# Squares of seven chunks added up on GpSimd, seven PSUM banks for the first feed-forward, wider mixer margins

## The chip, the cores and the metric

The kernel runs on the eight cores of one Trainium2 chip, each with four of the 32 sequences and without any exchange between cores. The time is that of the device, in microseconds (us), of the slowest core.

## What is computed

A macaron layer on x of shape (32, 2048, 1024): feed-forward, mixer of two attention groups, feed-forward, final norm. Weights are float32 in memory and bfloat16 in the matmuls.

```
h = x
h = h + 0.5 * swiglu(rmsnorm(h, g_ffn1), w_ffn1_gate, w_ffn1_up, w_ffn1_down)
u = rmsnorm(h, g_mix);  p = u @ w_in
o = concat(rmsnorm(mla(p), g_out_mla), rmsnorm(swa(p), g_out_swa))   # 8 heads each
h = h + o @ w_o
h = h + 0.5 * swiglu(rmsnorm(h, g_ffn2), w_ffn2_gate, w_ffn2_up, w_ffn2_down)
out = rmsnorm(h, g_final)
# rmsnorm(x, g) = x * rsqrt(mean(x*x) + 1e-6) * g;  swiglu = (silu(x@wg) * (x@wu)) @ wd, width 2816
```

## The kernel before

A core works on 16 tiles (NT) of 512 tokens, four per sequence. h lies transposed: 8 chunks of 128 features by 512 tokens in float32, with three buffers for h. For each tile there are FFN 1 (f = 0), the mixer, FFN 2 (f = 1) and the final norm. An FFN has 22 gate/up items (8 + 8 matmuls of 128x128 by 512 columns, L570 for the very first eight of a phase, L565 for the rest; tanh on ScalarE L580, two passes on VectorE L584 and L587) in two halves of 12 and 10, and after each half eight down items (L597; L604 adds the result to h). u, the normed input of an FFN, has one buffer, so it can be written only when the last gate/up item of the phase before has read it; eight down items of ten matmuls come behind that. The first two tiles go through FFN 1 together, with weights that are cast from float32 by GpSimd's DMAs on the way, in four quarters.

The norm of h (`pre_u` ahead of an FFN, in `mixer`, and in `final_out`) has this form: ScalarE squares a chunk into one of two buffers (sqF or sqM; L526, L711, L632), and `stat_mm` (L448) adds it up over the features on TensorE, with four matmuls that have the squares as weights and one column of 1/1024 as the moving operand. Eight chunks accumulate in one PSUM bank. VectorE then takes the reciprocal root with `newton` (L406 to L416, eleven operations on 128x4), and `bcast` (L425 to L435) writes it into diagonal matrices (dgF or dgM) that two matmuls (L435) spread over all partitions. VectorE scales h with it: L533 writes u, L719 the mixer's um, L640 the output.

PSUM has eight banks: FFNs turn over 0 to 2 (`fbank`), the mixer 3 to 6 (`mbank`), the norms use 7.

The order on each engine is made in advance. Every operation carries a planned duration (MM = 0.2185 per matmul, `d_act`, `d_dve`), a latency after it (LAT, 0.3 for GpSimd) and a due time vt; `Graph.schedule` is a list scheduler that takes on each engine, of the operations whose inputs are there in the plan, the one with the lowest vt. An FFN's operations have the running position fpos as vt, `pre_u` is due 20 ahead of it, and a mixer's operations are spread evenly over a window that ends 14 ahead of the tile's FFN 2. From then on each engine works through its list in that order, with semaphores for true dependences. The sequence of phases is FFN 1 of tile n, FFN 2 of tile n-1, and so on; the mixer of n fills in between.

```
            G.op("pe", [skey, ("onesc", oc)], [P(bank)], mm, 0.14)          # stat_mm
...
            pre_u(n, 16 * f, u1, ukey1, fpos[0] - 20)
...
                win[n] = (max(prev, phase_at[(0, n, "e")]), phase_at[(1, n, "s")] - 14.0)
```

GpSimd has only DMAs in its queue: the casting loads of the start, the outputs (outT) and the loads of x.

## Time and profile before

| | |
|---|---|
| median of 3 runs | 4984.26 us (4982.69 to 4986.34) |
| profiled execution, its time | 4978.47 us |
| its span, slowest core (core 2) | 4976.9 us |
| spans of the eight cores | 4958.9 to 4976.9 us |
| TensorE busy | 4827.9 us, 29209 matmuls recorded |
| VectorE busy | 2795.0 us |
| ScalarE busy | 1895.0 us |
| GpSimd busy | 91.2 us, 154 instructions |

The profile is of the slowest core of one execution. Engines are PE (TensorE matmul), PEld (its weight loads), DVE (VectorE), ACT (ScalarE), POOL (GpSimd) and SP (the queue of most DMAs). A share of busy time is a mean over the whole span, while the start, the long middle and the end have different limits, so it is read by stretches. Matmuls overlap, so their durations add up to more than the time between their starts. A few per cent of the matmul records are missing from this trace (29209 matmuls against 29784 weight loads). A wait is put down to the operation that came last.

### The profile page before, as it was taken

How to read it: one execution, taken by the hardware profiler on the slowest of the kernel's cores; microseconds unless marked ns; L12 is line 12 of the kernel's file. 1: busy time of each engine (PE TensorE's matmuls, PEld its weight loads, DVE VectorE, ACT ScalarE, POOL GpSimd, SP SyncE). 2: the span in 40 equal slices, each digit the busy share in tenths (PEclk: the TensorE clock that was granted, in tenths of full speed). 3: DMA queues.
4: the chain of work that ended last, by engine and by line, in shares of the span. 5: the costliest groups of instructions: out<-in, count | busy, mean ns of one | idle time of the engine just before them, and what ended most of it. 6: DMA issues, size and time to landing. Idle time of an engine off the chain costs nothing.

```text
span 4976.9 us, 93066 instructions; the slowest of 8 cores (4958.9 to 4976.9 us)
## 1 busy us (share of the span) xinstructions
PE 4827.9 (97%) x29209; PEld 2350.5 (47%) x29784; DVE 2795.0 (56%) x6313; ACT 1895.0 (38%) x3567; POOL 91.2 (2%) x154
## 2 busy tenths in 40 slices
PE   7899999999999999999999999999999999999998
PEld 3344444445444444544544444454544444445444
DVE  4366565555665565564557555555555655555654
ACT  1124425335233342534524243352642423336541
POOL 1100000000000000000000000000000000000000
PEclk9999999999999999999999999999999999999999
DMA  9985754544445454444445445444444545443434
GB/s 180 191 211 123 191 171 124 171 136 147 143 142 178 141 163 149 151 142 131 154 143 178 144 134 174 137 155 147 133 152 141 174 146 177 136 144 110 128 108 143
DMA packets 259288, 751.85 MB, mean 151 GB/s; under 512 B 28320, under 2 KB 36640, under 8 KB 258464
## 3 DMA queue, kind: packets, MB, share of 16 engines
q1 hardware_dynamic: 229664, 648.78, 41.9%
q0 software_dynamic: 28864, 97.07, 8.5%
q8 instruction: 258, 4.23, 0.4%
q14 instruction: 214, 1.75, 0.1%
q10 hardware_dynamic: 288, 0.03, 0.0%
HBM read 716.99 MB, written 73.92 MB: 159 GB/s over the span
## 4 chain that ended last, share of the span: by engine, by line
PE 92%; DMA 4%; DVE 2%; issue 2%; ACT 0%; SPq 0%; DVEq 0%; ACTq 0%; POOLq 0%; POOL 0%
PE ps L565 46%; PE ps L597 23%; PE ps L732 5%; PE ps L886 5%; PE ps L1039 4%; PE ps L906 3%; DMA sb_h<-xT 1%; PE ps L939 1%; PE ps L824 1%; DVE sb_u L533 1%; PE ps L435 1%; PE ps L448 1%; DMA sb_slotB<-wd 1%; PE ps L570 1%; PE ps L965 1%
## 5 line engine op out<-in xcount | busy, mean ns | idle before, releaser
L565 PE MATMUL ps<-sb_u,sb_slotA 128*128 128x512 bf16 x10390 | 2569.7, 380 | 33.4 <-DMA sb_slotA<-wgu 4.1
L565 PEld LDWEIGHTS ps<-sb_u,sb_slotA 128*128 128x128 bf16 x10688 | 999.1, 98 | 1077.2 <-issue 34.5
L597 PE MATMUL ps<-sb_act,sb_slotB 128*128 128x512 bf16 x5473 | 1311.0, 380 | 16.6 <-DMA sb_slotB<-wd 4.7
L584 DVE SCALAR_TENSOR_TENSOR sb_tb<-sb_tb,ps 128x512 f32<-128x512 f32 x704 | 483.0, 686 | 722.8 <-PE ps L565 322.6
L580 ACT ACTIVATE sb_tb<-ps 128x512 f32<-128x512 f32 x704 | 419.6, 596 | 1151.3 <-PE ps L565 927.5
L891 ACT ACTIVATE sb_PT<-ps 128x512 bf16<-128x512 f32 (+3 forms) x1280 | 653.4, 533 | 506.1 <-PE ps L886 364.0
L597 PEld LDWEIGHTS ps<-sb_act,sb_slotB 128*128 128x128 bf16 x5632 | 536.2, 98 | 608.4 <-issue 17.1
L587 DVE TENSOR_TENSOR sb_act<-sb_tb,ps 128x512 bf16<-128x512 f32 x704 | 482.7, 686 | 251.1 <-PE ps L565 212.5
L604 DVE SCALAR_TENSOR_TENSOR sb_h<-ps,sb_h 128x512 f32<-128x512 f32 x544 | 375.0, 690 | 409.2 <-PE ps L597 347.7
L886 PE MATMUL ps<-sb_QT,sb_KT 128*128 128x512 bf16 (+3 forms) x1225 | 407.1, 346 | 1.9 <-ACT sb_PT L891 0.7
L906 PEld LDWEIGHTS ps<-sb_VA,sb_PT 128*128 128x128 bf16 x4352 | 253.5, 98 | 193.4
L906 PE MATMUL ps<-sb_VA,sb_PT 128*128 128x65 bf16 x4352 | 294.5, 193 | 1.3
L732 PE MATMUL ps<-sb_um,sb_slotM 128*128 128x512 bf16 x1105 | 273.0, 380 | 7.3 <-DMA sb_slotM<-wms 6.4
L526 ACT ACTIVATE sb_sqF<-sb_h 128x512 bf16<-128x512 f32 x256 | 154.8, 626 | 246.9 <-PE ps L448 103.3
L1039 PE MATMUL ps<-sb_uo,sb_slotM 128*128 128x512 bf16 x962 | 229.8, 379 | 1.4 <-DVE sb_h L1043 0.4
L949 ACT ACTIVATE sb_PT<-ps 128x512 bf16<-128x512 f32 x248 | 146.0, 596 | 188.7 <-DVE ps L943 102.0
L943 DVE SCALAR_TENSOR_TENSOR ps<-ps,sb_Bb 128x512 f32<-128x512 f32 x248 | 169.3, 693 | 39.8 <-PE ps L939 38.1
L894 DVE TENSOR_TENSOR sb_PT<-sb_PT,sb_cmin 128x128 bf16<-128x128 bf16 x512 | 107.8, 221 | 138.4 <-ACT sb_PT L891 134.9
L533 DVE SCALAR_TENSOR_TENSOR sb_u<-sb_h,sb_gains,ps 128x512 bf16<-128x512 f32 x256 | 176.4, 740 | 10.2 <-PE ps L435 6.3
L732 PEld LDWEIGHTS ps<-sb_um,sb_slotM 128*128 128x128 bf16 x1112 | 108.8, 98 | 139.2 <-issue 9.5
L1043 DVE TENSOR_TENSOR sb_h<-ps,sb_h 128x512 f32<-128x512 f32 x128 | 88.4, 691 | 143.6 <-PE ps L1039 108.8
L886 PEld LDWEIGHTS ps<-sb_QT,sb_KT 128*128 128x128 bf16 x1280 | 124.4, 97 | 83.4 <-issue 1.8
(118 smaller groups left out, 2908.7 us busy)
## 6 DMA issues: line engine op xcount, KB each, us to landing
sb_slotA<-wgu2s SPq DMA_DIRECT2D x340, 512.0 KB, 3.5
sb_slotA<-wgu1s SPq DMA_DIRECT2D x308, 512.0 KB, 3.7
sb_slotM<-wms SPq DMA_DIRECT2D x318, 256.0 KB, 2.8
sb_slotB<-wd2s SPq DMA_DIRECT2D x120, 384.0 KB, 3.2
sb_slotB<-wd1s SPq DMA_DIRECT2D x112, 384.0 KB, 3.1
sb_slotB<-wd2s SPq DMA_DIRECT2D x124, 320.0 KB, 2.9
sb_slotB<-wd1s SPq DMA_DIRECT2D x112, 320.0 KB, 2.9
outT<-sb_h POOLq DMA_DIRECT2D x30, 1024.0 KB, 7.9
```

The source lines that it names most:

```text
L533: G.op("dve", [hk(n, kc), P(7), ("gains",)], ukey(kc), lambda kc=kc: nc.vector.scalar_tensor_tensor(out=ub[:, kc, :], in0=hc[:, kc, :], sc ...
L565: inst = nc.tensor.matmul(PS[bank][:], lhsT=w[:, a, kc, :], rhs=ub[:, kc, :], start=(kc == 0), stop=(kc == 7))
L580: G.op("act", [P(gb)], [("tb", t)], lambda: nc.scalar.activation(out=tb[:, t, :], in_=PS[gb][:], func=AF.Tanh, scale=0.5), d_act(512), vt=dv)
L584: G.op("dve", [("tb", t), P(gb)], [("tb", t)], lambda: nc.vector.scalar_tensor_tensor(out=tb[:, t, :], in0=tb[:, t, :], scalar=1.0, in1=PS ...
L587: G.op("dve", [("tb", t), P(ubk)], ak, lambda: nc.vector.tensor_tensor(out=act1[:, a0 + i, :], in0=tb[:, t, :], in1=PS[ubk][:], op=ALU.mul ...
L597: inst = nc.tensor.matmul(PS[bank][:], lhsT=w[:, c, :], rhs=act1[:, a0 + c, :], start=(c == 0), stop=(c == nch - 1))
L604: G.op("dve", [P(bank), hk(n, dc)], [hk(n, dc)], lambda: nc.vector.scalar_tensor_tensor(out=hc[:, dc, :], in0=PS[bank][:], scalar=0.25, in ...
L732: inst = nc.tensor.matmul(PS[b][:], lhsT=w[:, kc, :], rhs=um[:, kc, :], start=(kc == 0), stop=(kc == 7))
L886: G.op("pe", ktk(kti, hd) + [("Y", hd, 0), ("Y", hd, 1)], [P(b)], lambda: nc.tensor.matmul(PS[b][:, 0:N], lhsT=KT[:, kti, hd, kk * 128:(kk ...
L891: G.op("act", [P(b)], [("X", ps)], lambda: nc.scalar.activation(out=PT[:, ps, 0:N], in_=PS[b][:, 0:N], func=AF.Exp, scale=SC_MLA), d_act(N))
L906: inst = nc.tensor.matmul(PS[ob][:, j * 65:(j + 1) * 65], lhsT=PT[:, ps, (j - j0) * 128:(j - j0 + 1) * 128], rhs=VA[:, kb, hd, :], start=( ...
L1039: inst = nc.tensor.matmul(PS[b][:], lhsT=w[:, kc, :], rhs=uo[:, kc, :], start=(kc == 0), stop=(kc == 7))
```

## The change

A new function `h_stats` replaces the three places where squares went straight to TensorE. With `direct` nothing changes. Without it, the squares of chunks 0 and 1 are added on GpSimd into a float32 accumulator, those of chunks 2 to 5 are added to it one by one, and chunk 6 is added with the result in bfloat16 over the square itself; four matmuls take this sum of seven chunks and four more take chunk 7. The accumulator acF shares the place of dgF, and the mixer uses t2, the second half of wt. `direct` holds for tiles 0 and 1 ahead of FFN 1, for tiles 0, 1, 14 and 15 ahead of FFN 2 and in the mixer, and for the last output. While the first two tiles are in FFN 1, `fbank` turns over seven banks (0 to 6) in all quarters but the last. A mixer's window ends 45 ahead of FFN 2 for tile 0, 30 for tile 1 and 28 for the others, but for tiles 14 and 15, whose windows are set apart and stay; `pre_u` is due 24 ahead. GpSimd's addition is planned at D_POOL = 1.25. Behind the new function the lines of the changed kernel have higher numbers: stat_mm is L452, the additions are L468, L471 and L474, bcast's matmul is L439, L595 and L590 are gate/up and L622 is down.

```diff
--- before.py
+++ after.py
@@ -32,10 +32,12 @@
 NMP = 21
 NHS = 3
 FG = 2
+MARG = {0: 45.0, 1: 30.0}
 MAGIC = 1597463007.0
 
 
 MM = 0.2185
+D_POOL = 1.25
 LAT = {"pe": 0.33, "act": 0.22, "dve": 0.18, "pool": 0.3}
 SLACK_M = 0.6
 SLACK_E = 0.2
@@ -327,7 +329,9 @@
         Bb = sb("Bb", [128, 2, 8, 128], F32)
         sqF = sb("sqF", [128, 2, T], BF16)
         sqM = sb("sqM", [128, 2, T], BF16)
+        aF = here()
         dgF = sb("dgF", [128, 2, 4, 128], BF16)
+        acF = sb("acF", [128, T], F32, at=aF)
         dgM = sb("dgM", [128, 1, 4, 128], BF16)
         gains = sb("gains", [128, 43], F32)
         esink = sb("esink", [128, 8], F32)
@@ -451,6 +455,28 @@
                 return inst
             G.op("pe", [skey, ("onesc", oc)], [P(bank)], mm, 0.14)
 
+        def h_stats(n, sq, skey, acc, akey, bank, direct=False):
+
+            hc = h[n % NHS]
+            for c in range(8):
+                s = c % 2
+                G.op("act", [hk(n, c)], [(skey, s)], lambda c=c, s=s: nc.scalar.activation(
+                    out=sq[:, s, :], in_=hc[:, c, :], func=AF.Square), d_act(512))
+                if direct:
+                    stat_mm(sq, s, (skey, s), bank, 0, c == 0, c == 7)
+                elif c == 1:
+                    G.op("pool", [(skey, 0), (skey, 1)], akey, lambda: nc.gpsimd.tensor_tensor(
+                        out=acc, in0=sq[:, 0, :], in1=sq[:, 1, :], op=ALU.add), D_POOL)
+                elif 1 < c < 6:
+                    G.op("pool", [(skey, s)] + akey, akey, lambda s=s: nc.gpsimd.tensor_tensor(
+                        out=acc, in0=sq[:, s, :], in1=acc, op=ALU.add), D_POOL)
+                elif c == 6:
+                    G.op("pool", [(skey, 0)] + akey, [(skey, 0)], lambda: nc.gpsimd.tensor_tensor(
+                        out=sq[:, 0, :], in0=sq[:, 0, :], in1=acc, op=ALU.add), D_POOL)
+                    stat_mm(sq, 0, (skey, 0), bank, 0, True, False)
+                elif c == 7:
+                    stat_mm(sq, 1, (skey, 1), bank, 0, False, True)
+
 
         fpos = [0.0]
         phase_at = {}
@@ -458,8 +484,10 @@
         b_cnt = [0]
         f_bank = [0]
 
+        f_wide = [3]
+
         def fbank():
-            b = f_bank[0] % 3
+            b = f_bank[0] % f_wide[0]
             f_bank[0] += 1
             return b
 
@@ -517,15 +545,11 @@
             G.op("pe", reads, writes, fn, nmm * MM, vt=fpos[0] if vt is None else vt)
             fpos[0] += nmm * MM
 
-        def pre_u(n, gcol, ub, ukey, vt):
+        def pre_u(n, gcol, ub, ukey, vt, direct=False):
 
             G.vt = vt
             hc = h[n % NHS]
-            for c in range(8):
-                s = c % 2
-                G.op("act", [hk(n, c)], [("sqF", s)], lambda c=c, s=s: nc.scalar.activation(
-                    out=sqF[:, s, :], in_=hc[:, c, :], func=AF.Square), d_act(512))
-                stat_mm(sqF, s, ("sqF", s), 7, 0, c == 0, c == 7)
+            h_stats(n, sqF, "sqF", acF[:], [("dgF", 0), ("dgF", 1)], 7, direct)
             eps_in(PS[7][:, 0:4], [P(7)], nwF, 4, "nwF")
             newton(None, nwF, 4, "nwF")
             bcast(nwF, nwFb, "nwF", 0, 7, ("dgF",), dgF)
@@ -551,6 +575,7 @@
 
             def step(k, n, ub, uk, a0):
                 kind, grp, i = items[k]
+                f_wide[0] = 7 if len(tiles) > 1 and grp is not groups[-1] else 3
                 c_lo, nch = grp[0], grp[1]
                 view, keys = slots[k]
                 hc = h[n % NHS]
@@ -627,11 +652,7 @@
             si, ti = divmod(n, NTI)
             G.vt = vt
             hc = h[n % NHS]
-            for c in range(8):
-                s = c % 2
-                G.op("act", [hk(n, c)], [("sqF", s)], lambda c=c, s=s: nc.scalar.activation(
-                    out=sqF[:, s, :], in_=hc[:, c, :], func=AF.Square), d_act(512))
-                stat_mm(sqF, s, ("sqF", s), 7, 0, c == 0, c == 7)
+            h_stats(n, sqF, "sqF", acF[:], [("dgF", 0), ("dgF", 1)], 7, last)
             eps_in(PS[7][:, 0:4], [P(7)], nwF, 4, "nwF")
             newton(None, nwF, 4, "nwF")
             bcast(nwF, nwFb, "nwF", 0, 7, ("dgF",), dgF)
@@ -706,11 +727,7 @@
             R = [("R", j) for j in range(4)]
             G.dma("sp", "rope", [("pace", 0, 0, 16)] if n == 0 else [], [R[0], R[1]], rope[:].rearrange("p a t -> p (a t)"), rope_in[ti], 524288)
             bst = mbank()
-            for c in range(8):
-                s = c % 2
-                G.op("act", [hk(n, c)], [("sqM", s)], lambda c=c, s=s: nc.scalar.activation(
-                    out=sqM[:, s, :], in_=hc[:, c, :], func=AF.Square), d_act(512))
-                stat_mm(sqM, s, ("sqM", s), bst, 0, c == 0, c == 7)
+            h_stats(n, sqM, "sqM", t2, [W1], bst, n < 2 or n >= NT - 2)
             eps_in(PS[bst][:, 0:4], [P(bst)], nwM, 4, "nwM")
             newton(None, nwM, 4, "nwM")
             bcast(nwM, nwMb, "nwM", 0, bst, ("dgM",), dgM)
@@ -1069,13 +1086,13 @@
 
         late = [("A", i) for i in range(12, NFC)] + [("B", i) for i in range(8, 16)]
         PA, PB = late[:8], late[8:14]
-        pre_u(0, 0, u1, ukey1, -2000)
+        pre_u(0, 0, u1, ukey1, -2000, True)
         first_deps.update({0: [hk(0, 4)], 1: [hk(0, 5)], 2: [hk(0, 7)]})
         first_deps.update({i: [hk(1, min(7, 2 * i - 5))] for i in range(3, 8)})
 
         def second():
             load_x(1, 4, "sp", -4900, [hk(0, 7)])
-            pre_u(1, 0, u2, ukey2, -1500)
+            pre_u(1, 0, u2, ukey2, -1500, True)
         ffn(0, [one(0), two(1, 6)], QUARTERS, 3, {2: second})
         cast_first[0] = False
         a_ring[0] = ring_a
@@ -1103,7 +1120,7 @@
             if f == 1:
                 mixer(n)
                 m_cast[0] = False
-            pre_u(n, 16 * f, u1, ukey1, fpos[0] - 20)
+            pre_u(n, 16 * f, u1, ukey1, fpos[0] - 24, f == 1 and (n < 2 or n >= NT - 2))
             flush()
             b0 = fpos[0]
             lead[0] = LEAD_E if (f, n) in ((0, 2), (1, 0), (1, NT - 3), (1, NT - 2)) else 1000.0
@@ -1129,7 +1146,7 @@
         prev = 0.0
         for n in sorted(by_m):
             if n not in win:
-                win[n] = (max(prev, phase_at[(0, n, "e")]), phase_at[(1, n, "s")] - 14.0)
+                win[n] = (max(prev, phase_at[(0, n, "e")]), phase_at[(1, n, "s")] - MARG.get(n, 28.0))
             w0, w1 = win[n]
             prev = w1
             tot = 0.0
```

**What moves on TensorE at the start of FFN 2.** TensorE's rows at the end of an FFN 1 phase and the start of the FFN 2 phase behind it, in the middle of the program (a tile with the longest attention). sb_dgF is the diagonal matrix of the norm ahead of FFN 2, sb_sqM the squares of the next mixer's norm, sb_slotB_* down weights, sb_slotA_* gate/up weights. Before:

```order
L597 MATMUL ps<-sb_act,sb_slotB_72 128x512 x10
L435 MATMUL ps<-sb_dgF,sb_onesb 128x512
L597 MATMUL ps<-sb_act,sb_slotB_70 128x512 x5
L435 MATMUL ps<-sb_dgF,sb_onesb 128x512
L597 MATMUL ps<-sb_act,sb_slotB_70 128x512 x5
L448 MATMUL ps<-sb_onesc,sb_sqM 128x1 x4
L570 MATMUL ps<-sb_u,sb_slotA_68 128x512
L448 MATMUL ps<-sb_onesc,sb_sqM 128x1 x4
```

and with the change:

```order
L439 MATMUL ps<-sb_dgF,sb_onesb 128x512
L622 MATMUL ps<-sb_act,sb_slotB_72 128x512 x3
L439 MATMUL ps<-sb_dgF,sb_onesb 128x512
L622 MATMUL ps<-sb_act,sb_slotB_70 128x512 x10
L622 MATMUL ps<-sb_act,sb_slotB_71 128x512 x10
L622 MATMUL ps<-sb_act,sb_slotB_72 128x512 x10
L622 MATMUL ps<-sb_act,sb_slotB_70 128x512 x10
L622 MATMUL ps<-sb_act,sb_slotB_71 128x512 x10
L622 MATMUL ps<-sb_act,sb_slotB_72 128x512 x10
L622 MATMUL ps<-sb_act,sb_slotB_70 128x512 x10
L595 MATMUL ps<-sb_u,sb_slotA_68 128x512 x8
L590 MATMUL ps<-sb_u,sb_slotA_68 128x512 x8
```

The second dgF matmul has moved from five matmuls ahead of the first one that reads u to seventy ahead, and the groups of mixer squares that stood between the eight L570 have gone behind them.

**What moves on TensorE in the first feed-forward pair.** The squares of tile 2 (sb_sqF) and what stands around them; sb_slotK_* are four more gate/up buffers. Before, at the turn from the second to the third quarter:

```order
L597 MATMUL ps<-sb_act,sb_slotB_72 128x512 x12
L565 MATMUL ps<-sb_u,sb_slotK_95 128x512 x8
L448 MATMUL ps<-sb_onesc,sb_sqF 128x1 x12
L565 MATMUL ps<-sb_u,sb_slotK_96 128x512 x8
L448 MATMUL ps<-sb_onesc,sb_sqF 128x1 x8
L597 MATMUL ps<-sb_act,sb_slotB_71 128x512 x6
L448 MATMUL ps<-sb_onesc,sb_sqF 128x1 x4
```

and with the change, at the turn from the third to the fourth:

```order
L622 MATMUL ps<-sb_act,sb_slotB_72 128x512 x10
L622 MATMUL ps<-sb_act,sb_slotB_70 128x512 x10
L590 MATMUL ps<-sb_u_94,sb_slotA_67 128x512 x8
L452 MATMUL ps<-sb_onesc,sb_sqF 128x1 x8
L439 MATMUL ps<-sb_dgF,sb_onesb 128x512 x2
L622 MATMUL ps<-sb_act,sb_slotB_71 128x512 x17
```

They have moved back by some thirty rows, about a quarter of the pair, and the two dgF matmuls follow them at once.

**What GpSimd's queue holds in the middle of the program.** One output, the load of x behind it and the chain that comes next; sb_acF and sb_wt are the accumulators. Before, only the DMAs stood there. With the change:

```order
L474 TENSOR_TENSOR sb_sqF<-sb_sqF,sb_acF 128x512
L247 DMA outT<-sb_h_45 128x4x512 x2
L247 DMA sb_h_45<-xT 128x8x512
L468 TENSOR_TENSOR sb_acF<-sb_sqF 128x512
L471 TENSOR_TENSOR sb_acF<-sb_sqF,sb_acF 128x512 x4
L474 TENSOR_TENSOR sb_sqF<-sb_sqF,sb_acF 128x512
```

The six additions of a norm stand behind the load of x, which waits for the output ahead of it.

## Rows read from the trace of the kernel before

**Rows 1.** The page: busy time, and the chain that ended last, by engine.
```profile
PE 4827.9 (97%) x29209; PEld 2350.5 (47%) x29784; DVE 2795.0 (56%) x6313; ACT 1895.0 (38%) x3567; POOL 91.2 (2%) x154
...
PE 92%; DMA 4%; DVE 2%; issue 2%; ACT 0%; SPq 0%; DVEq 0%; ACTq 0%; POOLq 0%; POOL 0%
```

**Rows 2.** Stretches: length, busy us by engine, TensorE's clock, DMA share, GB/s.
```profile
150.00:250.00 100.00, 80.07 (x346) 34.04 (x352) 37.95 (x64) 11.42 (x20) 14.76 (x28) 0.88 0.92 196
...
600.00:700.00 100.00, 89.80 (x580) 43.10 (x591) 63.47 (x165) 42.63 (x82) 2.11 (x4) 0.93 0.45 127
...
800.00:4400.00 3600.00, 3566.34 (x21697) 1746.84 (x22124) 2042.21 (x4624) 1400.44 (x2620) 28.97 (x36) 1.00 0.48 150
...
1320.00:1325.00 5.00, 3.77 (x20) 1.91 (x22) 3.43 (x6) 2.85 (x5) 0.00 (x0) 0.67 0.17 66
```

**Rows 3.** TensorE's waits, 20 to 340 us: total us, times, longest.
```profile
PE ps L448 <- ACT sb_sqF L526: 10.0, 5, 5.4
PE ps L565 <- DVE sb_tb L584: 8.0, 5, 2.4
...
PE ps L597 <- DVE sb_h L604: 3.4, 3, 1.7
PE ps L597 <- DMA sb_slotB<-wd: 2.8, 2, 2.3
...
PE ps L565 <- DVE sb_h L604: 2.2, 2, 1.1
```

**Rows 4.** TensorE's waits, 340 to 800 us.
```profile
PE ps L732 <- DMA sb_slotM<-wms: 5.2, 2, 3.1
...
PE ps L570 <- DVE sb_u L533: 2.7, 7, 1.1
PE ps L448 <- ACT sb_sqM L711: 2.6, 6, 0.8
...
PE ps L435 <- DVE sb_dgF L432: 2.4, 1, 2.4
```

**Rows 5.** TensorE's waits, 800 to 4400 us.
```profile
PE ps L570 <- DVE sb_u L533: 7.7, 25, 0.7
PE ps L448 <- issue: 1.1, 3, 0.4
```

**Rows 6.** TensorE's waits, 4400 to 4977 us.
```profile
PE ps L435 <- DVE sb_dgF L432: 7.8, 3, 4.7
```

**Rows 7.** Groups of TensorE instructions by form: the stat matmuls.
```profile
L448 PE MATMUL ps<-sb_onesc,sb_sqF 128*128 128x1 bf16 x1536 | 83.3, 164 | 25.9 <-ACT sb_sqF L526 22.6 <-ACT sb_sqF L632 1.7 <-DVE sb_nwM L416 0.8
...
L448 PE MATMUL ps<-sb_onesc,sb_sqM 128*128 128x1 bf16 x704 | 41.1, 164 | 4.7 <-ACT sb_sqM L711 2.6 <-issue 1.1 <-ACT sb_sqM L755 0.9
```

**Rows 8.** TensorE's timeline, 1301 to 1324 us: start, length, operation, count.
```profile
1302.98 0.24 PE L448 MATMUL ps<-sb_onesc,sb_sqF 128*128 128x1 bf16 x4
1303.09 0.81 PE L1039 MATMUL ps<-sb_uo,sb_slotM 128*128 128x512 bf16 x3
1303.95 0.24 PE L448 MATMUL ps<-sb_onesc,sb_sqF 128*128 128x1 bf16 x4
1304.05 1.89 PE L1039 MATMUL ps<-sb_uo,sb_slotM 128*128 128x512 bf16 x8
1305.78 1.24 PE L597 MATMUL ps<-sb_act,sb_slotB 128*128 128x512 bf16 x5
```

**Rows 9.** Groups of VectorE and ScalarE instructions by form: busy us, mean ns.
```profile
L533 DVE SCALAR_TENSOR_TENSOR sb_u<-sb_h,sb_gains,ps 128x512 bf16<-128x512 f32 x256 | 176.4, 740 | 10.2 <-PE ps L435 6.3 <-PE ps L886 2.0 <-PE ps L906 1.7
...
L835 DVE TENSOR_TENSOR sb_qr<-sb_wt 128x512 bf16<-128x512 f32 x32 | 22.0, 687 | 1.8
...
L1092 DVE TENSOR_TENSOR sb_Bb<-sb_Bb,sb_mi 128x2048 f32<-128x2048 f32 x1 | 2.3, 2291 | 3.6 <-DMA sb_Bb<-bt 3.6
...
L526 ACT ACTIVATE sb_sqF<-sb_h 128x512 bf16<-128x512 f32 x256 | 154.8, 626 | 246.9 <-PE ps L448 103.3 <-DVE sb_h L1043 90.6 <-DMA sb_h<-xT 42.3
```

**Rows 10.** GpSimd's waits, the whole span.
```profile
POOL sb_h L245 <- DMA outT<-sb_h: 83.0, 10, 10.6
```

## The prediction

> **What bounds the kernel now.** First the page: TensorE is busy for 97% of the span and holds 92% of the chain that ended last [rows 1]. So a microsecond counts only if an instruction or a wait leaves TensorE's own queue. Second, the stretches [rows 2]: from 800 to 4400 us TensorE is busy for 3566 of 3600; time is lost ahead of 340 us, between 600 and 700, and behind 4400. The DMA engines are 92% busy between 150 and 250 us and 48% in the long middle. Third, TensorE's waits by stretch. In the first pair of feed-forwards it waits for squares, for PSUM banks that VectorE has not emptied (sb_tb, sb_h), but only 2.8 us for weights [rows 3]. From 340 to 800 it waits for the mixer's weights and for squares, dgF and u [rows 4]; in the middle almost only for u [rows 5]; at the end for dgF [rows 6].
>
> **Matmuls that go.** Before, 64 norms of h send eight squares each to TensorE, four 1-column matmuls per square (2048), and 16 mixers add 12 each for their latent norms: 2240, as the rows count them [rows 7]. Eleven of the 64 keep that form (two at the start, four before FFN 2, four in mixers, the last one). The other 53 (14 before FFN 1, 12 before FFN 2, 12 in mixers, 15 final) keep two groups of eight: 53 x 24 = 1272 matmuls less. Their price is not the 164 ns duration of the row, since matmuls overlap, but the time from the start of a group to the start of what follows: 1302.98 to 1303.09 and 1303.95 to 1304.05, so 0.10 to 0.11 us for four; I take 0.103 [rows 8]. (In the same rows eight 512-column matmuls go from 1304.05 to 1305.78, 0.216 each.) 318 groups x 0.103 = **33 us**, all of it on the bounding engine; no other cover exists. If groups also stop waiting for their squares it is more; that is in the next terms.
>
> The Trainium skill, page "TensorE: Matmul & The Clock Gate", section "LDWEIGHTS (loading the stationary operand)", gives a weight load of 128 columns about 107 ns; if these loads set the pace, 1272 of them would be worth an estimated 136 us. The trace disagrees: four loads and four matmuls pass in 0.11 us.
>
> **The middle: margins.** The mixer of a tile now ends 28 us ahead of its FFN 2 instead of 14 and the norm is asked for 24 us ahead instead of 20. The order shows what this does: before, the last dgF matmul stood one group ahead of the first matmul of FFN 2, with mixer squares between the eight that wait for u; now seven groups of ten (70 x 0.216 = 15 us) stand between, and the eight come in one row. The chain from dgF to a full u is eight L533 of 0.74 us with up to seven L604 passes of about 0.7 between, about 11 us [rows 9], so it fits in 15. That takes the waits on u (7.7) and the 1.1 of issue between them [rows 5], and most of the half clock behind the gap: 0.67 granted between 1320 and 1325, 3.3 us at 1.2 GHz [rows 2], costing half of itself, three times in the trace. I take **12 us** (8.8 of waits, the rest of clock). The same move for the early tiles (45 and 30 us) takes from 340 to 800 the waits on dgF (2.4), squares (2.6) and u (2.7) [rows 4]; the stretch 600 to 700 had a clock of 0.93, 14 us at the low level [rows 2], part of it behind this gap. I take **9 us**. The weight waits (5.2) stay. At the end the windows of the last two tiles keep their 14 us, and of the three waits on dgF, 7.8 us, the longest is 4.7, which I put down to the last output norm, where nothing changes [rows 6]: **2 us**.
>
> **The start: seven banks.** The waits on sb_tb and sb_h, 8.0 + 3.4 + 2.2, are three banks turning over when FFN 1 has only gate and up matmuls to issue; seven banks take them away. The squares' 10.0 us are tile 2's, whose x lands late; in the new order their matmuls stand in the last quarter of the pair, so this goes too [rows 3]. Ceiling 23.6 us, and some clock. But the weights come next: at 92% DMA share [rows 2] there is about 8% of the 240 us from 100 to 340 to catch up in, 19 us, and in the new order the two dgF matmuls stand right behind the two stat groups with nothing between, so a Newton chain of fourteen small VectorE operations plus dgF, some 6 us, can lie open there. I take **8 us** (ends: nothing, and 24).
>
> **GpSimd's additions: new.** 318 additions of 128x512, six in a chain per norm, each waiting for the one before. No row has one. Lower bound: VectorE's addition of two such operands from SBUF, 0.69 us; upper: its addition of four times the size, 2.29 us [rows 9]. I take the kernel's own table, D_POOL = 1.25, because its neighbours in that table match rows (the square is planned at 0.62 and takes 0.63, a VectorE pass 0.69 and 0.69) [rows 9]. Busy time costs nothing on an idle GpSimd; what counts is lateness, since TensorE's order is fixed and plans the stat group 1.55 us per addition (1.25 + 0.30) after the chain starts. If a step takes longer, TensorE stands. GpSimd's queue also holds the outputs and the loads of x; a load waits up to 10.6 us for the output ahead of it [rows 10], but in the order the next chain comes some 100 us of matmuls later. At the start, casting loads stand behind six additions on tile 2's squares, but later in the order than the place where TensorE waited for these squares before, so x should be there. Nothing for both. I put **8 us** for lateness, 53 chains x 0.15.
>
> Sum: -33 - 12 - 9 - 2 - 8 + 8 = **-56 us**. The profiled execution took 4978.5 (span 4976.9), so 4922; the median of the runs is 5.8 above it, so **4928 us**, 1.1% faster. (About 0.2%, 10 us, is what a measurement of this kernel can tell from no change.)
>
> **Rivals.**
> 1. *Only the matmuls go.* DMA takes back the start and new short waits the margins' gain: -33 to -38, so 4946 to 4951. For it: the DMA share of the start. Against it: the waits on u are VectorE's and the order puts 15 us before them. 20%.
> 2. *GpSimd is late; slower.* Place: the stat groups of the 53 norms. Where squares are all there (14 norms before FFN 1) six steps count; in the other 39 the chunks come 1.73 us apart or more (eight matmuls of 0.216) and only the last step counts, until a step is longer than 1.73; then all do. With a step of 1.55 + d the cost is (84 + 39) x d, plus 195 x (d - 0.18) beyond. Against a gain of 64 without lateness it decides from d = 0.31, a step of 1.86: with half of the table's 0.30 between two additions, an addition of about 1.7 us. At the upper bound, 2.29 + 0.15 per step, d = 0.89: 109 + 138 = 247, less 64, so 5167. At 1.8 us (d = 0.40): 49 + 43 - 64 = +28, 5012. For it: no row of the operation, and VectorE is 57% busy beside it (2042 of 3600 us) [rows 2]. Against: the table. 10%.
> 3. *Everything comes.* All 24 us of the start and some 5 of its half clock instead of 8, no lateness: -85, near 4900; half of both, 4912. For it: weights cost only 2.8 us of waits there. 12%.
> 4. *No effect:* the groups' cost is hidden otherwise. The row of 0.11 us speaks against it. 3%.
>
> The Trainium skill, page "GPSIMD Engine Reference", sections "Elementwise — side-by-side cycle accounting" and "Key points", gives a two-input GpSimd operation about 2.6 cycles per element, an estimated 1.11 us for 512 elements before overhead, sends elementwise work to VectorE instead, and says that GpSimd contends with VectorE operations that read two SBUF tensors. By the cycles alone the plan's step holds and rival 2 falls; by the contention it gains. No row here shows either.
>
> **Chances.** Forecast (4915 to 4942) 55%, rival 1 20%, rival 3 12%, rival 2 10%, rival 4 3%. Faster by over 0.2%: 0.87; within: 0.04; slower: 0.09. The range 4900 to 4962 takes in the forecast, rival 1 and most of rival 3, and leaves out rivals 2 and 4.
>
> **What would show it.** 968 stat matmuls on TensorE, and PE's waits from 800 to 4400 on u near nothing, with no half clock behind them. GpSimd with 318 TENSOR_TENSOR near 1.2 us each; waits of TensorE's stat line on GpSimd of under 10 us in all. No waits on sb_tb between 20 and 340, more on slotA or slotB. Wrong if the additions take over 1.7 us or stat matmuls wait on GpSimd by tens of microseconds, or if the first 340 us lose as much as before.

## The result, and the profile after

The change took **4912.7 us** (median of the first set of runs, 4895 to 4914; before 4985.1), 72 us less, where 56 were forecast; the ratio over these executions is **0.9844 [0.9818, 0.9871]**. A second set, the same kernel at another time (first experiment below), gave 4897 us and 0.9815 [0.9797, 0.9832], about 90 us less than before. Medians and ratios here and below leave out executions in which a die had a lower clock throughout. Part of the difference between the two sets is one stretch of 160 us in the profiled execution of the first, in which cores 0, 1, 6 and 7 had a clock of 0.81: they ended at 4907 to 4911 us, the other four at 4881 to 4885.

The page of the change, its slowest core: busy time, and the chain that ended last, by engine (before: [rows 1]).

```profile
PE 4832.4 (98%) x28512; PEld 2318.2 (47%) x28512; DVE 2803.2 (57%) x6313; ACT 1904.4 (39%) x3567; POOL 457.3 (9%) x472
...
PE 95%; DMA 3%; DVE 1%; issue 1%; POOL 0%; SPq 0%; ACT 0%; DVEq 0%; POOLq 0%; ACTq 0%
```

TensorE's part of the last chain went from 92% to 95%. The stretches of the change, core 1 (length; busy us of PE, PEld, DVE, ACT, POOL; granted clock; DMA share; GB/s). The same stretches of before are in [rows 2].

```profile
150.00:250.00 100.00, 87.22 (x365) 37.28 (x364) 40.95 (x69) 13.55 (x23) 21.71 (x34) 0.87 1.03 213
600.00:700.00 100.00, 99.58 (x595) 47.66 (x594) 75.42 (x202) 41.89 (x77) 16.06 (x16) 1.00 0.58 162
800.00:4400.00 3600.00, 3599.40 (x21208) 1735.24 (x21206) 2085.61 (x4711) 1411.82 (x2624) 353.30 (x318) 1.00 0.49 152
1320.00:1325.00 5.00, 5.00 (x25) 2.27 (x24) 3.26 (x5) 0.02 (x1) 0.00 (x0) 1.00 0.35 105
224.00:384.00 160.00, 158.64 (x709) 68.66 (x708) 92.79 (x178) 40.64 (x76) 8.37 (x16) 0.81 0.72 185
```

And the last of them on core 2 of the same execution:

```profile
224.00:384.00 160.00, 157.03 (x888) 74.33 (x887) 111.32 (x232) 56.54 (x114) 8.89 (x17) 1.00 0.78 205
```

In the long middle TensorE now stands still for 0.6 us of 3600, and the stretch 600 to 700 has its full clock. For before, [rows 2] is not the right row to compare with: it is of core 2, whose trace lacks 2% of the matmul records there (21697 matmuls beside 22124 weight loads). Core 1 of the same execution is complete, and idle for 10.6:

```profile
800.00:4400.00 3600.00, 3589.41 (x22114) 1745.39 (x22112) 2042.57 (x4623) 1399.99 (x2618) 28.98 (x36) 1.00 0.48 150
```

From 224 to 384 us, core 1 of the change got 709 matmuls through and core 2 888; it ended 28 us later.

TensorE's waits after, four stretches (20 to 340, 340 to 800, 800 to 4400, 4400 to 4977 us), total, times, longest. Before: [rows 3 to 6].

```profile
PE ps L590 <- DVE sb_tb L609: 8.3, 2, 8.0
PE ps L439 <- DVE sb_dgF L436: 4.8, 1, 4.8
PE ps L595 <- DVE sb_u L557: 1.6, 3, 1.2
...
PE ps L749 <- DMA sb_slotM<-wms: 11.8, 2, 6.1
...
PE ps L595 <- DVE sb_u L557: 1.3, 3, 0.6
...
PE ps L1056 <- DMA sb_slotM<-wms: 0.3, 1, 0.3
...
PE ps L439 <- DVE sb_dgF L436: 8.7, 2, 4.7
PE ps L885 <- DVE sb_KT L880: 2.2, 3, 0.9
```

GpSimd's additions, groups by form (busy us, mean ns | idle before):

```profile
L471 POOL TENSOR_TENSOR sb_acF<-sb_sqF,sb_acF 128x512 f32<-128x512 bf16 x164 | 190.7, 1163 | 190.2 <-ACT sb_sqF L463 186.3
L471 POOL TENSOR_TENSOR sb_wt<-sb_sqM,sb_wt 128x512 f32<-128x512 bf16 x48 | 55.9, 1165 | 3.6 <-ACT sb_sqM L463 1.9
L474 POOL TENSOR_TENSOR sb_sqF<-sb_sqF,sb_acF 128x512 bf16<-128x512 bf16 x41 | 47.7, 1163 | 58.8 <-ACT sb_sqF L463 58.2
...
L468 POOL TENSOR_TENSOR sb_acF<-sb_sqF 128x512 f32<-128x512 bf16 x41 | 47.3, 1155 | 3072.1 <-ACT sb_sqF L463 982.3 <-PE ps L1056 763.9 <-PE ps L439 560.3
```

An addition takes 1.16 us; the plan had counted 1.25 and 0.30 of latency, a step of 1.55. From start to start, an addition that reads the result of the one just before it comes 1.30 us behind it at the earliest, so this is the real step of a chain; where additions of two chains alternate, starts are 1.12 us apart. No wait of TensorE on GpSimd is in the lists, on any core. The estimate of 1.11 us worked out in the prediction from the Trainium skill, page "GPSIMD Engine Reference", section "Elementwise — side-by-side cycle accounting", stands 5% under the 1.16 of the rows: it agrees.

**Where the time went, by stretch.** The floor is the sum over TensorE's matmuls of the usual spacing of their starts where nothing waits: columns at 2.4 GHz plus 2.8 ns (0.216 us for 512), and 25 ns for one column. Lost time is what the spacing of their starts has beyond it, waits and low clock together, taken as the mean over the cores whose records are complete (us).

| Run | Floor | 0 to 340 | 340 to 800 | 800 to 4350 | 4350 to end |
|---|---|---|---|---|---|
| before | 4808.8 | 58.5 | 38.8 | 17.9 | 27.5 |
| the change, first set | 4777.0 | 46.9 | 29.0 | -1.8 | 25.6 |
| the change, second set | 4777.0 | 42.6 | 25.5 | -1.8 | 26.2 |

(-1.8 of 3550 is how exact the floor is.) From before to the second set: 32 matmuls, 16 the start, 13 the stretch to 800, 20 the middle, 1 the end, together 82; the spans of the slowest cores (4976.9 and 4895.4) differ by the same 82. (The second set's own comparison gives 93, 4990 less 4897: the profiled execution of before is from the first set, and with 4978 it was faster than the other four there.)

### The profile page after: what moved, and what is told of

Read it like the earlier page. It is cut to its first block, busy times and chain, and to the rows that moved or that the text cites. A ratio compares the mean times of both kernels' runs of the same rounds, so it can differ in the third digit from the quotient of the medians.

```text
span 4911.1 us, 91964 instructions; the slowest of 8 cores (4880.6 to 4911.1 us)
## 1 busy us (share of the span) xinstructions
PE 4832.4 (98%) x28512; PEld 2318.2 (47%) x28512; DVE 2803.2 (57%) x6313; ACT 1904.4 (39%) x3567; POOL 457.3 (9%) x472
## 3 DMA queue, kind: packets, MB, share of 16 engines
q1 hardware_dynamic: 229664, 648.78, 42.6%
## 4 chain that ended last, share of the span: by engine, by line
PE 95%; DMA 3%; DVE 1%; issue 1%; POOL 0%; SPq 0%; ACT 0%; DVEq 0%; POOLq 0%; ACTq 0%
PE ps L590 47%; PE ps L622 24%; PE ps L749 5%; PE ps L903 5%; PE ps L1056 4%; PE ps L923 3%; PE ps L841 1%; PE ps L956 1%; PE ps L595 1%; PE ps L439 1%; DMA wd1s<-sb_slotB 1%; PE ps L982 1%; PE ps L813 1%; PE ps L1030 1%; DMA sb_slotM<-wms 0%
## 5 line engine op out<-in xcount | busy, mean ns | idle before, releaser
L590 PE MATMUL ps<-sb_u,sb_slotA 128*128 128x512 bf16 x10688 | 2605.6, 381 | 1.0 <-DVE sb_PT L911 0.3
L590 PEld LDWEIGHTS ps<-sb_u,sb_slotA 128*128 128x128 bf16 x10688 | 1007.9, 98 | 1090.1 <-issue 48.4
L622 PE MATMUL ps<-sb_act,sb_slotB 128*128 128x512 bf16 x5632 | 1324.3, 381 | 2.6 <-DMA sb_slotB<-wd 1.4
L609 DVE SCALAR_TENSOR_TENSOR sb_tb<-sb_tb,ps 128x512 f32<-128x512 f32 x704 | 483.4, 687 | 634.7 <-PE ps L590 324.9
L622 PEld LDWEIGHTS ps<-sb_act,sb_slotB 128*128 128x128 bf16 x5632 | 539.3, 98 | 615.9 <-issue 26.3
L903 PE MATMUL ps<-sb_QT,sb_KT 128*128 128x512 bf16 (+3 forms) x1280 | 426.5, 348 | 0.2
L463 ACT ACTIVATE sb_sqF<-sb_h 128x512 bf16<-128x512 f32 x384 | 236.3, 626 | 364.1 <-DVE sb_h L1060 168.0
L468 POOL TENSOR_TENSOR sb_acF<-sb_sqF 128x512 f32<-128x512 bf16 x41 | 47.3, 1155 | 3072.1 <-ACT sb_sqF L463 982.3
L749 PE MATMUL ps<-sb_um,sb_slotM 128*128 128x512 bf16 x1112 | 276.6, 384 | 13.1 <-DMA sb_slotM<-wms 11.8
L471 POOL TENSOR_TENSOR sb_acF<-sb_sqF,sb_acF 128x512 f32<-128x512 bf16 x164 | 190.7, 1163 | 190.2 <-ACT sb_sqF L463 186.3
L911 DVE TENSOR_TENSOR sb_PT<-sb_PT,sb_cmin 128x128 bf16<-128x128 bf16 x512 | 119.1, 244 | 140.8 <-ACT sb_PT L908 136.9
```

Of the source, the lines that this page charges most:

```text
L463: G.op("act", [hk(n, c)], [(skey, s)], lambda c=c, s=s: nc.scalar.activation(out=sq[:, s, :], in_=hc[:, c, :], func=AF.Square), d_act(512))
L590: inst = nc.tensor.matmul(PS[bank][:], lhsT=w[:, a, kc, :], rhs=ub[:, kc, :], start=(kc == 0), stop=(kc == 7))
L609: G.op("dve", [("tb", t), P(gb)], [("tb", t)], lambda: nc.vector.scalar_tensor_tensor(out=tb[:, t, :], in0=tb[:, t, :], scalar=1.0, in1=PS ...
L622: inst = nc.tensor.matmul(PS[bank][:], lhsT=w[:, c, :], rhs=act1[:, a0 + c, :], start=(c == 0), stop=(c == nch - 1))
L749: inst = nc.tensor.matmul(PS[b][:], lhsT=w[:, kc, :], rhs=um[:, kc, :], start=(kc == 0), stop=(kc == 7))
L903: G.op("pe", ktk(kti, hd) + [("Y", hd, 0), ("Y", hd, 1)], [P(b)], lambda: nc.tensor.matmul(PS[b][:, 0:N], lhsT=KT[:, kti, hd, kk * 128:(kk ...
```

## Experiments

All edits are made to the changed kernel, unless a sentence says otherwise. Each set of runs had the kernel before beside it on the same chip. Times over the change are against the second set.

### The change again

The changed kernel without an edit, the reference for the next three.

> The changed kernel again, unaltered, beside the kernel before on the same chip. In its profile cores 0, 1, 6 and 7 had a stretch of 160 us from 223 us on with a granted clock of 0.81 and ended 25 us behind the other four (4881 to 4885). If that stretch belongs to the kernel's order, some cores show it in nearly every execution and the slowest core is near 4911; if it is chance of the execution, executions without it end near 4890. Ratio to before 0.982 to 0.986 either way.

Measured: 4897 us (4892 to 4900) against 4990 for before on that chip, ratio 0.9815 [0.9797, 0.9832]. The change is worth some 90 us where no stretch at 0.81 falls into it; the profiled execution has none on any core, so the kernel's order does not bring it by itself.

### All squares back on TensorE

```
 def h_stats(...):
-                if direct:
+                if True:
```

> The change with every norm's squares straight to TensorE (no addition on GpSimd); seven banks and margins stay. Theory: the 1272 matmuls come back at 0.103 us per four, +33 us, less the 8 us stall of 164 us, in which ScalarE's tanh stands behind squares that wait for GpSimd: undisturbed cores near 4884 + 25 = 4909, 2240 stat matmuls. Rival: GpSimd's additions cost nothing at the start and save waits of the stat groups too, then +33 to +45 (4917 to 4929).

Measured: 4941 us, 0.9904 [0.9889, 0.992]: 44 us over the change. The floor is 31.8 us higher, and lost time is 43.1, 34.3, 0.0 and 31.5 by stretch. So the margins alone clear the middle: TensorE is busy 3597.95 of 3600 us there. The rest is in the stretch to 800 (9 more than in the second set) and the end (5); since two profiles of one kernel differ by 3.5 and 0.6 there, how much of these is the edit's stays open. The GpSimd part carries about half of the change's 90 us, once margins and banks are there.

### Old margins

```
-MARG = {0: 45.0, 1: 30.0}
+MARG = {}
...
-            pre_u(n, 16 * f, u1, ukey1, fpos[0] - 24, ...)
+            pre_u(n, 16 * f, u1, ukey1, fpos[0] - 20, ...)
...
-                win[n] = (..., phase_at[(1, n, "s")] - MARG.get(n, 28.0))
+                win[n] = (..., phase_at[(1, n, "s")] - MARG.get(n, 14.0))
```

> The change with the margins of before (14 for all tiles, norm due 20 ahead). Theory: the margins are worth 19 us from 800 to 4400 (waits on u and half clock behind them) and up to 19 between 340 and 800: undisturbed cores near 4884 + 30 = 4914, waits on u from 800 to 4400 back to 8 us or more. Rival: the fewer stat groups between the matmuls that read u did it, and the margins alone are worth under 10 us: 4884 to 4894. Second rival: with the old margins the longer GpSimd chain is late and it costs more than before, over 40 us.

Measured: 4952 us, 0.9927 [0.9911, 0.9943]: 55 us over the change. Lost time by stretch: 46.2, 34.7, 35.8, 33.6. TensorE's waits in it, 800 to 4400 us:

```profile
PE ps L595 <- DVE sb_u L557: 11.0, 32, 0.9
PE ps L439 <- DVE sb_dgF L436: 8.9, 12, 1.2
PE ps L452 <- DVE sb_u L557: 2.4, 6, 0.4
```

That is more than before had in the same stretch [rows 5], and there is a wait on dgF that before had none of. With the old margins the longer chain through GpSimd ends too late, and TensorE waits for what comes behind it (the Newton steps, dgF, u), not for the sum itself. The margins are worth 38 us in the middle with the GpSimd sums, and 18 without (before 17.9, all on TensorE with the new margins 0.0). They are two things at once: a gain of their own and the price of the GpSimd chain.

### Three banks for the first FFN

```
-                f_wide[0] = 7 if len(tiles) > 1 and grp is not groups[-1] else 3
+                f_wide[0] = 3
```

> The change with three banks for the first pair. Theory: the waits on sb_tb and sb_h of 13.6 us come back and part of the half clock, +10 to +20 on undisturbed cores (4894 to 4904). If the stretch of clock 0.81 comes from the denser start, it is absent here and the slowest core is no slower than 4904, so the kernel as a whole gains; rival: the stretch is as frequent here, slowest core 4920 to 4930.

Measured: 4911 us in two executions, 14 over the change; no interval. Lost time ahead of 340 us is 59.4 against 42.6, everything behind it as in the change. Its waits, 20 to 340 us:

```profile
PE ps L590 <- DVE sb_tb L609: 25.3, 6, 9.3
PE ps L590 <- DVE sb_h L629: 3.0, 3, 1.1
```

Three banks with the GpSimd sums lose as much at the start as before did (58.5), so the start's whole gain is the banks'.

### Tile 2's first norm without GpSimd

With seven banks a wait of 8 us on sb_tb was still there. The rows of the change around it, core 1: GpSimd, then ScalarE, then VectorE, then TensorE (start, length, operation, idle before and what ended it).

```profile
160.22 0.53 POOL L247 DMA_DIRECT2D sb_slotB<-wd  x1 [14.02 <-PE ps L622]
...
161.86 1.06 POOL L247 DMA_DIRECT2D sb_slotM<-wm  x2
162.92 1.18 POOL L468 TENSOR_TENSOR sb_acF<-sb_sqF 128x512 f32<-128x512 bf16 x1
...
164.20 1.15 ACT L463 ACTIVATE sb_sqF<-sb_h 128x512 bf16<-128x512 f32 x2 [12.78 <-POOL sb_acF L468]
...
169.83 0.58 ACT L605 ACTIVATE sb_tb<-ps 128x512 f32<-128x512 f32 x1
...
170.51 0.69 DVE L609 SCALAR_TENSOR_TENSOR sb_tb<-sb_tb,ps 128x512 f32<-128x512 f32 x1 [9.17 <-ACT sb_tb L605]
...
172.85 3.57 PE L590 MATMUL ps<-sb_u,sb_slotK 128*128 128x512 bf16 x8 [7.98 <-DVE sb_tb L609]
```

The first addition stands behind casting loads in GpSimd's queue, of which the first waits 14 us for its slot. The square buffers are two, so ScalarE's third square waits for the addition; the tanh stands behind the squares on ScalarE, VectorE's product behind the tanh, and TensorE runs out of banks. The edit takes this chain off GpSimd:

```
-            pre_u(n, 16 * f, u1, ukey1, fpos[0] - 24, f == 1 and (n < 2 or n >= NT - 2))
+            pre_u(n, 16 * f, u1, ukey1, fpos[0] - 24, (f, n) == (0, 2) or f == 1 and (n < 2 or n >= NT - 2))
```

> The change with tile 2's first statistics left on TensorE (the squares of h of tile 2, before the second pair of the first FFN): six additions fewer on GpSimd, six groups of four one-column matmuls more on TensorE (6 x 0.103 us = 0.6 us). Theory A (GpSimd's queue is what stalls the start): the third square there waited for the first addition, the addition stood behind casting loads in GpSimd's queue, the tanh behind the square on ScalarE, sb_tb behind the tanh, and PE 8 to 10 us for sb_tb. Without additions the squares wait for PE's groups alone: PE's longest wait on sb_tb in 20 to 340 us falls from 8 to 10 us to under 2, and the median to 4890 to 4895 (7 to 8 us under the change on the same day; the ratio to before 0.980). Theory B (the stall is that of tile 2's x, which comes late from memory): the squares wait as long for the x, the stall stays, and the time is that of the change or 0.6 us more.

Measured: 4897, 4900 and 4918 us, 0.9845 [0.9818, 0.9872], no gain over the change. Its waits, 20 to 340 us:

```profile
PE ps L622 <- DMA sb_slotB<-wd: 9.9, 3, 7.8
PE ps L439 <- DVE sb_dgF L436: 4.8, 1, 4.8
PE ps L590 <- DMA sb_slotA<-wgu1s: 4.1, 1, 4.1
```

The mechanism of theory A is right: sb_tb is gone from the list. Its size is not: TensorE, 8 us further on, meets a down-projection weight that is not there yet, for 7.8 us, and the stretch loses 45.1 us, as it did. In the change that wait was 1.1. The weight's own rows say why, core 5 of each: its load was issued at 186.7 us here and at 195.4 in the change (second set), and landed at 216.0 in both. So it is the transfer that sets the time there, with the DMA engines full (1.03 in the window above, from 150 to 250), and the 8 us stall in front of it was free.

### GpSimd's sums alone

The kernel **before** with the sums and nothing else; as an edit to the change it is the two diffs above, margins and banks, together.

> The kernel before with the GpSimd sums and nothing else: three banks, the mixer's work planned to end 14 us before the next phase, pre_u due 20 us ahead. Theory A (the additions lengthen the chain to u, and only the larger margins pay for that): this is the sum of the two parts undone singly, 53 us (margins) and 11 us (banks) over the change, 4950 to 4965 us, so 20 to 35 us under before although 32.8 us of matmuls are gone at the most; waits on sb_u and sb_dgF in 800 to 4400 us as in the run with the old margins, 20 us or more. Theory B (parts add up independently): before less 32 to 33 us, and no more than before's own waits in the middle (17.9 us lost there), 4950 to 4953. Under 4945 both fall.

Measured: 4966 us against 4984 for before, 0.9967 [0.995, 0.9985]: 18 us faster. Of 31.8 us of matmuls removed, 14 came back by these times and 19 by the profiled executions: lost time by stretch is 59.3, 35.5, 33.1, 33.4, that is 15 more than before in the middle, 6 more at the end and 3 less from 340 to 800. Its waits from 800 to 4400 us:

```profile
PE ps L595 <- DVE sb_u L557: 12.5, 39, 0.9
PE ps L439 <- DVE sb_dgF L436: 6.2, 8, 1.2
```

That is 1 us over theory A's upper end, and 13 us above theory B's. So: sums alone 0.33%, margins and banks alone 0.96% (all squares on TensorE, above), both 1.85%. The two add up to 1.29%; the other 0.56%, some 28 us, exists only where both are in. Lost time puts it in the middle (17 us), at the end (11) and from 340 to 800 (6), and hardly at the start (1), where the banks work; 35 by this measure. So it is the margins that hide the longer chain.

### All eight squares on GpSimd

```
                 elif c == 6:
-                    ... out=sq[:, 0, :], in0=sq[:, 0, :], in1=acc, op=ALU.add), D_POOL)
-                    stat_mm(sq, 0, (skey, 0), bank, 0, True, False)
+                    ... out=acc, in0=sq[:, 0, :], in1=acc, op=ALU.add), D_POOL)
                 elif c == 7:
-                    stat_mm(sq, 1, (skey, 1), bank, 0, False, True)
+                    ... out=sq[:, 1, :], in0=sq[:, 1, :], in1=acc, op=ALU.add), D_POOL)
+                    stat_mm(sq, 1, (skey, 1), bank, 0, True, True)
```

> The change with the eighth square added on GpSimd as well: one group of four one-column matmuls for each statistic in place of two (53 groups fewer, 53 x 0.103 = 5.5 us), seven additions of 1.16 us in place of six. Theory A (in the middle of the program GpSimd's chain has room to spare, lateness costs nothing): 5 us under the change, 4890 to 4896, with no wait on sb_sqF in 800 to 4400 us. Theory B (the chain is on the edge: one more addition of 1.16 us shows for each of the 53 chains): 53 x 1.16 = 61 us more than it saves, 4950 or so, with waits of the stat line on GpSimd. In between, a loss at the start and the end alone (four to six chains where PE has nothing else to do): the time of the change within 3 us.

Measured: 4893.6 us (4892 to 4904), 0.9821 [0.9806, 0.9835]; the change had 0.9815. Theory B, the chain at its edge, falls: there is no wait on squares or on GpSimd in the middle, and lost time there is -2.3. The floor is 5.3 us lower; 2.3 and 2.8 us more were lost in the two stretches ahead of 800 us, no more than profiled executions of one kernel differ there (4.3 and 3.5 us between the two of the change). To settle whether the 5 us arrive, both ran once more side by side.

> The change itself again, for a comparison with the next two on one chip at one time: 4892 to 4900 us in its fast executions, 0.981 to 0.983 of before. Both theories expect the same here; it gives the noise of the comparison.

> All eight squares added on GpSimd, again, beside the change. TensorE's floor is 5.3 us lower (4771.7 against 4777.0 us), but the first look gave 0.9821 of before against the change's 0.9815, and 2 to 3 us more lost time in each of the two stretches before 800 us. Theory A (that was the spread between executions): 4 to 6 us under the change in this call. Theory B (the start and the stretch to 800 us are paced by weight transfers, so matmuls saved there come back as waits on transfers, and only the matmuls saved in 800 to 4400 us count: 39 groups of 0.103 us): 4 us under. Theory C (the seventh addition costs the chains at the ends what the middle gains): within 2 us of the change.

Measured: 4890 us, one execution, for the change; 4885 and 4892 for all eight. The change ran in 4890 to 4900 in the second and third set, this kernel in 4885 to 4904. Whether it beats the change by the 4 to 5 us of the floor stays open: the measurement does not resolve it.

### Each addition twice

```
                 elif 1 < c < 6:
+                    ... out=acc, in0=sq[:, s, :], in1=acc, op=ALU.add), D_POOL - 0.3)
-                    ... out=acc, in0=sq[:, s, :], in1=acc, op=ALU.add), D_POOL)
+                    ... out=acc, in0=sq[:, s, :], in1=acc, op=ALU.add), 0.0)
```

and the same for chunk 6. The second addition counts each square twice, so the norms are other numbers; the planner's step stays 1.55 us, and 48 of the 53 groups that read a sum keep their place in TensorE's list.

> Each addition but a chain's first is made twice (the sums are then other numbers), while the planner is told the same 1.55 us for a step as in the change: a real step of 2 x 1.13 = 2.3 us. It tests the point from which a late GpSimd turns the change round. Theory A (PE waits one for one for what the chain is later than its plan): 5 x (2.3 - 1.55) = 3.6 us for each of 53 chains, 190 us over the change, 5090 us, and slower than before; PE waits of the stat line on POOL of 2 to 4 us each. Theory B (ScalarE's squares stand so far apart in the real run, or PE's stat groups so far behind, that the lateness is mostly hidden): under 50 us over the change, 4900 to 4950, and still faster than before; the waits are few. In neither case does the end of u's chain come late in the middle, since the margins are 28 us.

Measured: 5054.6 us, 1.0141 [1.0124, 1.0158]: 160 us over the change, slower than before. Lost time by stretch: 49.3, 40.6, 131.4, 36.1. TensorE's waits, 800 to 4400 us, core 7:

```profile
PE ps L452 <- POOL sb_sqM L478: 86.7, 10, 9.5
PE ps L452 <- POOL sb_sqF L478: 11.4, 10, 2.6
```

The total is near theory A, its distribution is not. Ten mixer norms wait 8.7 us each on average; of the output and FFN norms ten wait 0.3 to 2.6 us, 1.1 on average, the others not at all. The timeline before one of the long ones says why, GpSimd's rows and then TensorE's:

```profile
982.65 1.16 POOL L471 TENSOR_TENSOR sb_wt<-sb_sqM,sb_wt 128x512 f32<-128x512 bf16 x1
983.77 1.17 POOL L473 TENSOR_TENSOR sb_acF<-sb_sqF,sb_acF 128x512 f32<-128x512 bf16 x1
...
996.45 1.16 POOL L473 TENSOR_TENSOR sb_wt<-sb_sqM,sb_wt 128x512 f32<-128x512 bf16 x1
997.75 1.16 POOL L476 TENSOR_TENSOR sb_wt<-sb_sqM,sb_wt 128x512 f32<-128x512 bf16 x1
999.05 1.16 POOL L478 TENSOR_TENSOR sb_sqM<-sb_sqM,sb_wt 128x512 bf16<-128x512 bf16 x1
...
1000.36 0.24 PE L452 MATMUL ps<-sb_onesc,sb_sqM 128*128 128x1 bf16 x4 [9.51 <-POOL sb_sqM L478]
```

And the stretches around it:

```profile
990.00:1000.00 10.00, 0.84 (x4) 0.20 (x2) 0.69 (x1) 2.52 (x5) 9.43 (x9) 0.66 0.06 24
1000.00:1010.00 10.00, 9.64 (x46) 4.26 (x47) 5.38 (x19) 1.20 (x2) 0.21 (x1) 0.83 0.32 107
```

Two chains, one on acF and a mixer norm's on wt, take turns on GpSimd: 22 additions from 973 to 1000 us, 1.12 us from start to start where the chains alternate, and 1.30 where the mixer's stands alone at the end. So the real step of a doubled chain is 2.60 us by itself and some 4.5 beside another, where the expectation counted 2.3. And the stop costs twice: the clock falls, to a mean of 0.66 and 0.83 in the two windows, and matmuls run at the lower of the two levels (1.2 GHz) for a while behind the wait. The 98 us of listed waits are 33 less than the time lost in the stretch.

### A plan that is too early

```
-D_POOL = 1.25
+D_POOL = 0.6
```

> The change with the planner told 0.6 us for an addition in place of 1.25, so a planned step of 0.9 us where a real one takes 1.12 to 1.3: PE's stat groups stand up to 6 x 0.3 = 1.8 us too early in TensorE's order. Theory A (lateness costs PE one for one): 53 chains x 1.3 to 1.8 us = 70 to 95 us over the change. Theory B (as in the doubled run, the lateness is mostly hidden for the first FFN's and second FFN's chains, 1.1 us each there for 3.6 us, and shows for the 12 mixer chains only, since there two chains share GpSimd): 12 x 2 to 5 us, and under half a us for each of the others, 20 to 60 us over. Theory C (the plan's value is without effect): within 3 us of the change.

Measured: 4899 and 4903 us, 0.982 [0.9721, 0.992]. Lost time by stretch: 38.9, 30.9, -2.2, 29.4. Nothing in the middle, where the 12 mixer norms were to show; 5 us more than in the second set from 340 to 800 and 3 at the end, of which the wait list has

```profile
PE ps L452 <- POOL sb_sqF L474: 2.6, 2, 1.7
```

and 4 less at the start. Against the one execution of the change on the same chip (4890) it is 9 and 13 us slower, against the second set 2 and 6.

The kernel did not become what the expectation describes, so theories A and B are not tested by it. TensorE's list, counted in matmul time, has 46 of the 53 groups that read a sum at the same place as in the change; three in the middle stand 0.4 us earlier, one stands 3.5 later. The planned length of an addition hardly moves them. Only three groups came forward by more, 4.8, 2.2 and 3.9 us (at some 657, 4545 and 4755 us), and these are the ones at which TensorE waits for GpSimd: 0.7, 0.9 and 1.7 us on core 5. Theory C, within 3 us, stays open.

How far the change stands off its edge is read from its own trace instead. From the end of a chain's last addition to the first matmul that reads the sum, in 800 to 4400 us on core 1, the shortest time is 0.7 us and the median 7.4 for the output and FFN norms, and 2.0 to 4.6 us for the mixer norms. The doubled additions, five more per chain, used this up.

## Why the prediction was right, and where it was not

**Faster, 4900 to 4962.** The measured 4913 lies in it, though 2 us below the forecast's own bracket (4915 to 4942). That it does is in part luck: in the profiled execution the four cores without the stretch at 0.81 ended at 4881 to 4885, and the second and third set, 4890 to 4900, lie at the range's lower end or below it. The sum of -56 measures -82 between the profiled executions of before and of the second set: -32, -20, -13, -1, -16 and 0 for -33, -12, -9, -2, -8 and +8. Rival 3 stood near 4900, but it gave its extra gain to the start, and it came from all stretches.

**Matmuls, -33.** Measured -32: 968 stat matmuls, 552 and 416 in the two groups, and 31.8 us of floor. The whole of it arrives only if the chain behind the sum is hidden, which the term did not say.

**The middle, -12.** The mechanism is right: in the profiled execution of the change no wait on u is left in the middle, and core 1 has one unbroken stretch at full clock from 553 to 4772 us. The size was 20. The term that was mis-sized is "8.8 of waits, the rest of clock", in its waits. The list's idle time runs from the modelled end of the last matmul, and matmuls overlap, so each wait is listed too short. The timeline of before, TensorE, core 1:

```profile
1318.10 0.24 PE L448 MATMUL ps<-sb_onesc,sb_sqM 128*128 128x1 bf16 x4
1318.55 0.38 PE L570 MATMUL ps<-sb_u,sb_slotA 128*128 128x512 bf16 x1 [0.20 <-DVE sb_u L533]
```

Four stat matmuls take 0.103 us from start to start; here 0.45 pass, so 0.35 is lost and 0.20 is listed. The list of core 1 has 9.7 us in 34 waits, each listed 0.15 too short: that is 15 us, and the sample, core 2, had missing records as well. The spacing of starts is the right measure. Half clock is the smaller part, as forecast: core 1 has one such piece, 6.8 us, in the whole middle, which costs half of itself.

**340 to 800, -9.** Measured -13, and -10 in the first set. The clock is the larger part: time at half clock fell from 26.5 to 11.9 us (mean of the cores, second set), worth 7, and the stretch 600 to 700 went from 0.93 to 1.00. The weight waits did not stay at 5.2: they were 11.8 in the profiled run of the change.

**The end, -2.** Measured -1. The output norm's 4.7 stays, as said.

**The start, -8.** Measured -16 (-12 in the first set), all of it from seven banks (three banks: 59.4 lost, as before). The mis-sized step is that the weights would take back all but 8 of the 23.6 us. In the change TensorE waits 1 to 3 us for down weights and up to 5 for others, and time at half clock ahead of 340 us fell from 23.9 to 17.5 us (mean of the cores), worth 3. "No waits on sb_tb" failed: one of 8 us is there. The step that failed there is "x should be there. Nothing for both". The x was there; but the additions stood behind casting loads in GpSimd's queue, and ScalarE's squares, the tanh and VectorE behind them. I had asked what the queue does to the sum, and not what it does to the two square buffers. It cost nothing in the end, since a weight comes next that lands no earlier (tile 2's norm on TensorE: sb_tb gone, 7.8 us of wait for the weight). The new wait on dgF, foreseen at some 6 us, is 4.8.

**GpSimd's lateness, +8.** Measured 0. An addition took 1.16 us, inside 0.69 to 2.29 and near the 1.25 taken, and a step 1.30, less than the 1.55 planned; no wait on it shows. "53 chains x 0.15" put a price on chains that were done 0.7 us or more ahead of their reader in the middle. What the chain does cost is at its far end, in u, and there the margins pay.

**Rivals.** Rival 1 (-33 to -38) falls, but describes something real: with the sums alone it is less still, -18. Rival 2 did not come, but its side and place are confirmed by the doubled additions: slower, with stat matmuls waiting for GpSimd. Its formula gives, for the step of 2.60 us that a doubled chain shows by itself (d = 1.05), 129 + 170 = 299 over the change; measured 160. Its picture of evenly late norms was wrong: where two norms share GpSimd the wait is 8.7 us, elsewhere 1.1 or none. A straight line from the plan's 1.55 through this run crosses before's time at a step of about 2.15 us (an estimate from one run; 1.86 was given). Rival 4, no effect, falls: with the squares back on TensorE the floor is 31.8 us higher and the time 44.

## What to carry to other kernels

Moving work off the bounding engine onto an idle one lengthens a chain, and the gain arrives only as far as something pays for the length: here the same edit was worth 18 us alone and 44 with larger margins and seven banks. Sum the spacing of starts against a floor before costing a stretch, because a wait list understates each stop among pipelined matmuls (9.7 us listed, some 15 there). When an edit is to move operations in a plan, compare the order that comes out before reading its time (a planned step of 0.9 us left 46 of 53 groups in place). A stall ahead of a transfer that is late anyway costs nothing and its removal brings nothing; and when an operation is put in another queue, ask who shares its input buffers, not only who reads its result.
